# Attention by token tile with unnormalised P, and the convolution's inputs first in the odd projection

## What is computed

```python
z = h @ w_in
u_c = z[..., :2 * D_C]                              # 2 x 512, convolution: value and gate
q = rms_norm(z[..., o1:o2].reshape(B, T, 8, 64), q_g)
k = rms_norm(z[..., o2:o3].reshape(B, T, 2, 64), k_g)
v = z[..., o3:].reshape(B, T, 2, 64)
...
s = jnp.einsum('bqhgd,bkhd->bhgqk', qblk, k) * 64 ** -0.5
p = jax.nn.softmax(s, axis=-1)
o = jnp.einsum('bhgqk,bkhd->bqhgd', p, v)
...
g = val * jax.nn.sigmoid(gate)
y_c = silu(layer_norm(depthwise_conv(g, conv_w, conv_b, 15, 15)))   # 31 taps
y = jnp.concatenate([y_c, attn], axis=-1) @ w_out
```

## Time and profile before

| | |
|---|---|
| median of 3 runs | 2182.76 us (2178.67 to 2184.53) |
| the profiled execution | 2183.45 us, span 2181.8 us |
| TensorE busy | 1896.4 us, 87% of the span |
| DVE busy | 1391.6 us, 64% |
| ACT busy | 780.4 us, 36% |
| POOL busy | 268.7 us, 12% |
| chain that ended last | PE 73%, DVE 14%, issue 8%, ACT 2% |

### The profile page before, as it was taken

How to read it: one execution, slowest core, us unless ns; L and a number is a source line. 1 busy time by engine, 2 the same in 40 slices (tenths; PEclk the granted TensorE clock), 3 DMA queues, 4 the chain that set the end, 5 groups by cost and what they waited for, 6 DMA issues and landing times.

```text
span 2181.8 us, 34451 instructions
## 1 busy us (share of the span) xinstructions
PE 1896.4 (87%) x11818; PEld 1676.3 (77%) x11819; DVE 1391.6 (64%) x2732; ACT 780.4 (36%) x1297; POOL 268.7 (12%) x280
## 2 busy tenths in 40 slices
PE   4898899999999999977789767979797898797975
PEld 2694599999999999933336646979687898797974
DVE  1578745678888854389875472448576796684435
ACT  1425333221222223323323332336444565452321
POOL 1001100000000000089300010020101110101021
PEclk9999899999999999956779987989898998898996
DMA  7343224457744424200000132467757898866433
GB/s 225 116 150 121 78 75 121 134 153 231 205 136 125 148 66 138 69 19 3 0 1 10 36 106 80 118 188 211 207 158 208 244 253 242 232 177 174 116 90 129
DMA packets 439501, 288.76 MB, mean 132 GB/s; under 512 B 20858, under 2 KB 428634, under 8 KB 439300
## 3 DMA queue, kind: packets, MB, share of 16 engines
q1 hardware_dynamic: 425124, 248.75, 39.4%
q0 software_dynamic: 12272, 34.50, 5.1%
q10 hardware_dynamic: 1904, 3.13, 0.5%
HBM read 262.86 MB, written 23.47 MB: 131 GB/s over the span
## 4 chain that ended last, share of the span: by engine, by line
PE 73%; DVE 14%; issue 8%; ACT 2%; DMA 1%; ACTq 1%; DVEq 1%; POOL 0%; POOLq 0%
PE ps L1116 15%; PE ps L1117 15%; PE ps L1118 15%; PE ps L1121 11%; PE ps L1122 5%; DVE vp L2105 3%; PE ps L1228 2%; DVE lo L1727 2%; PE ps L1159 1%; PE ps L1441 1%; PE ps L1178 1%; PE ps L1458 1%; DVE am L2166 1%; DVE hot L2320 1%; ACT hi L700 1%
## 5 line engine op out<-in xcount | busy, mean ns | idle before, releaser
L700 ACT ACTIVATE hi<-raw 128x1024 fp32r<-128x1024 f32 (+3 forms) x442 | 397.1, 919 | 512.9 <-PE ps L1118 348.3
L1116 PE MATMUL ps<-h_wide,hi 128*128 128x320 f32 (+1 forms) x1728 | 542.2, 314 | 32.6 <-issue 26.5
L1117 PE MATMUL ps<-h_wide,hi 128*128 128x320 f32 (+1 forms) x1728 | 537.5, 311 | 0.0
L1118 PE MATMUL ps<-h_wide,lo 128*128 128x320 f32 (+1 forms) x1728 | 537.4, 311 | 0.0
L1727 DVE TENSOR_TENSOR lo<-raw,hi 128x1024 fp32r<-128x1024 f32 (+3 forms) x442 | 451.9, 1050 | 48.3 <-ACT hi L700 44.1
L1116 PEld LDWEIGHTS ps<-h_wide,hi 128*128 128x128 f32 x1728 | 327.8, 190 | 35.3 <-issue 33.1
L1121 PE MATMUL ps<-h_wide,hi 128*128 128x256 f32 (+2 forms) x1056 | 294.2, 364 | 61.8 <-issue 54.6
L1117 PEld LDWEIGHTS ps<-h_wide,hi 128*128 128x128 f32 x1728 | 327.4, 189 | 0.4 <-issue 0.2
L1118 PEld LDWEIGHTS ps<-h_wide,lo 128*128 128x128 f32 x1728 | 327.6, 190 | 0.0
L1121 PEld LDWEIGHTS ps<-h_wide,hi 128*128 128x128 f32 x1056 | 210.7, 200 | 68.5 <-issue 52.6
L1122 PE MATMUL ps<-h_wide,lo 128*128 128x128 f32 (+2 forms) x1056 | 258.0, 244 | 0.0
(11 more groups left out here) (337 smaller groups left out, 2459.2 us busy)
## 6 DMA issues: line engine op xcount, KB each, us to landing
raw<-in_moe_w_dram SPq DMA_DIRECT2D x160, 512.0 KB, 5.2
raw<-in_w_mod_dram SPq DMA_DIRECT2D x96, 512.0 KB, 4.6
raw<-in_moe_w_dram SPq DMA_DIRECT2D x64, 384.0 KB, 3.5
raw<-in_ff_w_dram SPq DMA_DIRECT2D x40, 512.0 KB, 4.7
raw<-in_moe_w_dram SPq DMA_DIRECT2D x64, 320.0 KB, 3.8
y_rows<-zeros POOLq DMA_DIRECT2D x22, 512.0 KB, 4.5
raw<-in_moe_w_dram SPq DMA_DIRECT2D x32, 256.0 KB, 2.9
raw<-in_ev_w_in_dram SPq DMA_DIRECT2D x12, 512.0 KB, 6.4
```

Source lines behind the costliest of these rows:

```text
L700: act.activation(hi[c % 2][:, parts[h]], raw[slot][:, parts[h]], ACT.Copy).then_inc(hi_done, 1)
L1116: pe.matmul(out, w_hi, v_hi, start=first, stop=False, skip_group_check=True)
L1117: pe.matmul(out, w_hi, v_lo, start=False, stop=False, skip_group_check=True)
L1118: return pe.matmul(out, w_lo, v_hi, start=False, stop=last, skip_group_check=True)
```

## The change

1. **Steps by token tile.** s = 8 t + h: first all eight heads of tile 0 (the context), then those of tile 1, and so on.
2. **P isn't divided.** ACT's exp takes P with scale -1 and the row minimum as bias (the q gain is multiplied by -1/8 once, at the start). The row sums of a tile's eight heads are kept, and the division is done on the output: `rows_out(t)` takes one reciprocal of eight and eight multiplications of 128 x 64, from PSUM. DVE's negation, reciprocal, multiplication of P and copy of the fifth tile are gone; ACT copies all five transposed tiles at once.
3. **P·V the other way round.** `weigh(s)` comes three steps behind the scores: P's transpose (128 x 128) is the weight, five of them a step (one for tile 0), and 64 columns of V are streamed, so queries are on the partitions of the result. `turn_back(t)` transposes a tile's 128 x 512 result with four transposes, and `rows_hi` and `rows_lo` write its high and low parts. Banks alternate by tile.
4. **The odd projection's order** is values and gates of the convolution first (chunks 3, 5, 4, 6), then q, k and v. DVE multiplies values by gates (`gated`) and does 22 taps between the chunks. POOL still waits for all four groups.

```diff
+ODD = (3, 5, 4, 6, 0, 1, 2)
...
-            for c in range(7):
-                split_hi(OIN + c + 2)
-                in_place(6 + c, c, z_odd)
+            for p in range(7):
+                split_hi(OIN + p + 2)
+                in_place(6 + p, ODD[p], z_odd)
...
             def kept(s):
 
-                h, t = s // TT, s % TT
                 act.wait_ge(a_t, s + 1)
-                if h >= 2:
-                    act.wait_ge(a_pv, h - 1)
-                if t == 0:
-                    act.activation(ptp[:, h % 2, :], ps[:, 4, 0:P], ACT.Copy).then_inc(a_kept, 1)
+                if s >= 2:
+                    act.wait_ge(a_pvs, s - 1)
+                if s < NH:
+                    act.activation(pt[:, s % 2, 0, :], ps[:, 4, 0:P], ACT.Copy).then_inc(a_kept, 1)
                 else:
-                    act.activation(pt[h % 2][:, 0:4, (t - 1) * P:t * P], ps[:, 4, 0:512].rearrange("p (k c) -> p k c", k=4),
+                    act.activation(pt[:, s % 2].rearrange("p k c -> p (k c)"), ps[:, 4:6, :].rearrange("p a b -> p (a b)")[:, 0:T],
                                    ACT.Copy).then_inc(a_kept, 1)
...
+            def rows_hi(t):
+                act.wait_ge(a_back, t + 1)
+                act.activation(hh[:, NC:KT, t * P:(t + 1) * P], ps[:, 6 + t % 2, :].rearrange("p (j c) -> p j c", j=NC), ACT.Copy).then_inc(a_ohi, 1)
...
-                    act.activation(dst, src, ACT.Exp, scale=HD ** -0.5, bias=am[:, 1, s % 2:s % 2 + 1],
-                                   accum_out=am[:, 2, s % 2:s % 2 + 1]).then_inc(a_exp, 1)
+                    if h == 0 and t >= 2:
+                        act.wait_ge(a_rows, t - 1)
...
+                    act.activation(dst, src, ACT.Exp, scale=-1.0, bias=am[:, t % 2, 0, h:h + 1],
+                                   accum_out=am[:, t % 2, 1, h:h + 1]).then_inc(a_exp, 1)
...
+            def weigh(s):
+
+                t, h = s // NH, s % NH
                 r = slice(HD * (h // 4), HD * (h // 4) + HD)
-                if k == 0:
-                    pe.wait_ge(a_kept, TT * (h + 1))
-                    pe.wait_ge(a_kept5, (TT - 1) * (h + 1))
-                    if h:
-                        pe.wait_ge(a_ohi, h)
-                        pe.wait_ge(a_olo, h)
-                    pe.matmul(ps[r, 7, 0:TP], vt[:, 0, r], ptp[:, h % 2, :], start=True, stop=True)
-                last = pe.matmul(ps[r, 6, 0:TS], vt[:, 1 + k, r], pt[h % 2][:, k, :], start=k == 0, stop=k == 4, skip_group_check=True)
-                if k == 4:
-                    last.then_inc(a_pv, 1)
+                at = P * (h % 4) + HD * (h // 4)
+                pe.wait_ge(a_kept, s + 1)
+                if h == 0 and t >= 2:
+                    pe.wait_ge(a_olo, t - 1)
+                tiles = 1 if t == 0 else 5
+                for k in range(tiles):
+                    last = pe.matmul(ps[:, 6 + t % 2, at:at + HD], pt[:, s % 2, k, :], vt[:, k if t == 0 else 1 + k, r], start=k == 0, stop=k == tiles - 1, skip_group_check=True)
+                last.then_inc(a_pvs, 1)
+
+            def turn_back(t):
+
+                pe.wait_ge(a_rows, t + 1)
+                for j in range(NC):
+                    last = pe.transpose(ps[:, 6 + t % 2, j * P:(j + 1) * P], o_rows[:, t % 2, j * P:(j + 1) * P], ident)
+                last.then_inc(a_back, 1)
...
-                if s >= 7:
-                    weigh((s - 7) // TT, (s - 7) % TT)
+                if 3 <= s < NH * TT + 3:
+                    weigh(s - 3)
+                if s >= NH + 5 and (s - 5) % NH == 0:
+                    turn_back((s - 5) // NH - 1)
...
+            dve.tensor_scalar(par[:, 1, QN:QN + 1], par[:, 1, QN:QN + 1], -HD ** -0.5, None, ALU.mult)
...
+            for p in range(7):
+                raw_out(6 + p, OIN + p, ODD[p], z_odd)
+                split_lo(OIN + p + 2)
+                if p in (2, 4):
+                    gated(p - 2)
+                    gated(p - 1)
+                if p >= 2:
+                    taps((4, 7, 4, 7, 0)[p - 2])
...
+            def rows_out(t):
+
+                slot = t % 2
+                dve.wait_ge(a_exp, NH * (t + 1))
+                link(dve.reciprocal(am[:, slot, 2, :], am[:, slot, 1, :]))
+                dve.wait_ge(a_pvs, NH * (t + 1))
+                if t >= 2:
+                    dve.wait_ge(a_back, t - 1)
+                for h in range(NH):
+                    at = P * (h % 4) + HD * (h // 4)
+                    last = dve.tensor_scalar(o_rows[:, slot, at:at + HD], ps[:, 6 + slot, at:at + HD], am[:, slot, 2, h:h + 1], None, ALU.mult)
+                last.then_inc(a_rows, 1)
...
+                if s >= NH + 4 and (s - 4) % NH == 0:
+                    rows_out((s - 4) // NH - 1)
+                if s >= NH + 7 and (s - 7) % NH == 0:
+                    rows_lo((s - 7) // NH - 1)
                 taps(2)
```

More of the change, by code:

```diff
@@ L76, in among @@
     return BY_PE.index(q) if q in BY_PE else q - sum(p < q for p in BY_PE)
-MANY = [(ring_of(OIN + c), 3) for c in range(2)] + [(ring_of(OOUT + c), 1) for c in range(4)]
+ODD = (3, 5, 4, 6, 0, 1, 2)
+MANY = [(ring_of(OIN + ODD.index(c)), 3) for c in range(2)] + [(ring_of(OOUT + c), 1) for c in range(4)]
 def landed(r):
@@ L365, in hybrid_trunk_step @@
         a_exp = sem("a_exp")
-        a_norm = sem("a_norm")
         a_t = sem("a_t")
         a_kept = sem("a_kept")
-        a_kept5 = sem("a_kept5")
-        a_pv = sem("a_pv")
+        a_pvs = sem("a_pvs")
+        a_rows = sem("a_rows")
+        a_back = sem("a_back")
         a_ohi = sem("a_ohi")
@@ L602, in q_columns, with odd_columns @@
                      src[:, k:k + 4, e, 2 * c + j, :]) for k in (0, 4) for j in range(2) for e in range(2)]
-            for c in range(2):
-                load(OIN + c, q_columns(c))
+            def odd_columns(c):
+                return q_columns(c) if c < 2 else columns(w, 2 * D_A + 512) if c == 2 else columns(w, (c - 3) * 256)
+            for p in range(2):
+                load(OIN + p, odd_columns(ODD[p]))
             sp.wait_ge(evac, 2 * OIN)
@@ L612, in _ @@
             sp.dma_start(hspread[:, :, :], a["const_hspread"]).then_inc(odd_in, 16)
-            load(OIN + 2, columns(w, 2 * D_A + 512))
-            for c in range(3, 7):
-                load(OIN + c, columns(w, (c - 3) * 256))
+            for p in range(2, 7):
+                load(OIN + p, odd_columns(ODD[p]))
             wo = a["od_w_out"][0]
@@ L1417, in turn @@
             def turn(s):
-                pe.wait_ge(a_norm, s + 1)
+                pe.wait_ge(a_exp, s + 1)
                 if s:
                     pe.wait_ge(a_kept, s)
[L1422 to L1427, removed]
+                for k in range(1 if s < NH else 5):
@@ L1445, in _ @@
+            def turn_back(t):
[3 more added lines that the diff above has]
+                last.then_inc(a_back, 1)
             pe.wait_ge(v_kept, 2)
             pe.wait_ge(o_rope, 5)
-            for s in range(NH * TT + 7):
-                if s < NH * TT:
-                    h, t = s // TT, s % TT
+            for s in range(NH * TT + 6):
+                t, h = s // NH, s % NH
+                if t < TT:
@@ L2080, in z_odd @@
                 return gp[:, m - 10, p0 + lo_t:p0 + hi_t]
[L2082 to L2093, removed]
             conv_w = GC_W - 30
@@ L2111, in taps, with gated @@
                 del todo[:n]
+            def gated(c):
+                dve.wait_ge(in_kept, 2 * (6 + 2 * (c // 2 + 1)))
+                for lo_t, hi_t, cond in SEGS:
+                    p0 = (GC_P, GC_S)[cond]
+                    last = dve.tensor_tensor(gp[:, c, p0:p0 + hi_t - lo_t], gp[:, c, p0:p0 + hi_t - lo_t], vp[:, c, lo_t:hi_t], ALU.mult)
+                last.then_inc(gp_set, 1)
+            dve.wait_ge(gp_pads, 1)
+            for p in range(7):
[6 more added lines that the diff above has]
+                    taps((4, 7, 4, 7, 0)[p - 2])
             taps(4)
@@ L2168, in _ @@
-                if 1 <= s < NH * TT + 1:
-                    u = s - 1
-                    width = P if u % TT == 0 else T
-                    dve.wait_ge(a_exp, u + 1)
-                    link(dve.reciprocal(am[:, 3, u % 2:u % 2 + 1], am[:, 2, u % 2:u % 2 + 1]))
-                    dve.tensor_scalar(pp[:, u % 2, 0:width], pp[:, u % 2, 0:width], am[:, 3, u % 2:u % 2 + 1], None, ALU.mult).then_inc(a_norm, 1)
-                if 2 <= s < NH * TT + 2 and (s - 2) % TT:
-                    u = s - 2
-                    h, t = u // TT, u % TT
-                    dve.wait_ge(a_t, u + 1)
-                    if h >= 2:
-                        dve.wait_ge(a_pv, h - 1)
-                    dve.tensor_copy(pt[h % 2][:, 4, (t - 1) * P:t * P], ps[:, 5, 0:P]).then_inc(a_kept5, 1)
@@ L2181, in _ @@
-                if s >= 12 and (s - 2) % TT == 0:
-                    head_lo((s - 12) // TT)
+                    if h == 0 and t >= 2:
+                        dve.wait_ge(a_exp, NH * (t - 1))
+                    low = am[:, t % 2, 0, h:h + 1]
+                    if t == 0:
```

(3 more changed lines are left out.)

50 lines of the change are left out of this document (19 added, 31 removed).

## The result

The changed kernel takes 2203.34 us (median of 7 runs, 2197.3 to 2208.56) against 2182.76 (7 runs, 2176.56 to 2189.86) beside it: ratio 1.0094, 95% interval 1.007 to 1.0117. It is 20.6 us slower; 2212 was forecast, 29 us slower, in a range of 2177 to 2227. The profiled execution has a span of 2201.7 us.

What follows compares the result with a forecast made beforehand. The prediction took TensorE as the bound, at a low clock in attention. Last scores +27.6 us and tail +1.5 made +29.1 on the profiled 2183.45 us: 2212 us, range 2177 to 2227.

Steps and rivals of the forecast that it cites:

- The clock: Attention: mixture too lean, so granted clock stays 0.50 from 945 to past the last scores, though TensorE never pauses.
- Rival 1: Attention: full clock is granted in tile 1 and stays, steps about 3.35 us, 2131 us in all; chance 0.11.
- A reading behind it: Before the attention, 945 to 967: TensorE busy 20.9 of 22 us, nearly all with 10-row weights, without the clock rising.
- The product: P·V in a full-tile step: ten load-bound records cost 2.3 us at 1.2 GHz, against 1.90 before.
- Rival 2: P·V product: loads hide in the streams, 1.26 us at 1.2 GHz, 2179 us in all, no change; chance 0.06.
- The transposes: Attention step: five transposes of P cost 1.26 us at 1.2 GHz, within a step of 5.99.
- the mark: Attention's end, the start of DVE's first mean subtraction: 1166.26 before, forecast 29.1 us later.
- Tile 0: Attention's first eight steps: 2.6 us each, 20.8 in all, with 2.18 for two convolution taps beside POOL.
- The tail: Last scores to DVE's first mean subtraction: 21.9 us against 20.4 before, +1.5.
- The projection: Odd projection's new order: last chunk's first half evicted some 4 us later, covered; were that cover gone, 1 to 4 us.
- The order's gain: Odd projection: the gatings leave the stage's end, but DVE waited there for the q/k sums anyway: nothing gained.
- The break-even: Attention: the change breaks even where 20 of the 32 long steps run at the low clock; below that it is faster.

Runs made afterwards that it cites:

- experiments 2 and 3: Changed kernel with 128 instead of 64 columns streamed per product record, in all heads or half; versions computing the whole attention took 2139.78 and 2147.54 us.
- burst_late_lo: Changed kernel plus eight extra fp32 512-column matmuls once, at tile 1's first product, and DVE's low part one step later; 2134.02 us in one run.
- experiment 6: As burst_late_lo, but four extra matmuls instead of eight; median 2175.62 us over ten executions.
- burst: Changed kernel plus eight extra fp32 512-column matmuls into a free bank, once, at tile 1's first product; 2193.9 us in one run.
- half_wide: Changed kernel with heads 0 to 3 streaming all 128 columns of V, heads 4 to 7 writing over the useless half; 2147.54 us, ratio to before 0.9828.
- late_lo: Changed kernel with only DVE's low part of a tile one step later, no extra matmuls; 2200.04 us in one run.
- burst4_late_lo: The kernel of experiment 6: four extra matmuls against eight in burst_late_lo; two executions of 2118 and 2124 us, eight of 2174 to 2183.
- wide_pairs: Changed kernel streaming V beside 64 zero columns, heads ordered 0, 4, 1, 5, ... so sharers of a PSUM stretch follow each other; 2139.78 us, ratio to before 0.9805.
- wide_v: Changed kernel streaming V beside 64 zero columns, head order unchanged; output differs; 2277.69 us, not comparable, first mean subtraction at 1122.40 instead of 1189.03.

## Why the forecast was right, and where it wasn't

- **The clock.** Right: 0.50 from the QK norm to past the last scores, with TensorE never idle from 1010 on. The reason held too: more columns behind the same loads bring it back (experiments 2 and 3). What the forecast lacked is that the level has a memory. It said that the mixture is too lean; the runs say that it is too lean to raise the clock from 0.50, but can keep it once it is up: from 1011 to 1090 in `burst_late_lo`, but not in every execution (experiment 6). Rival 1 (granted in tile 1 and kept) was thus nearer than its 0.11 and the reading of the earlier trace rows made it look: one burst and one wait away, in the executions that kept the clock. In the changed kernel as it stands a pause as in `burst` would probably have ended it.
- **A reading behind it.** One of the forecast's rows doesn't say what it took from it. TensorE's busy time in 945 to 967 isn't nearly all with 10-row weights: groups of that window, before the change, are

```profile
L1398 PE MATMUL ps<-hrs,hspread 10*128 10x320 f32 x19 | 11.4, 761 | 0.0
L1406 PE MATMUL ps<-qf,mats 128*128 128x512 f32 x8 | 8.3, 1142 | 0.0
```

  and 2.0 us more of the second kind for the keys. So about half of it was long streams through 128 rows, and the clock didn't rise. The experiments carry the conclusion without this row, but what exactly the clock follows stays open.
- **The product.** 2.16 us a step against 2.3, within its bounds of 1.26 and 2.5. Rival 2, loads hidden in the streams, falls: ten records take 1.23 us with 64 columns and 1.28 with 128, so the load is what is paid. The Trainium skill (TensorE: Matmul & The Clock Gate, LDWEIGHTS (loading the stationary operand)) would have a load of 128 columns in P / 1.2 ns, an estimate of 107 ns. The trace disagrees at the low clock and is near it at the high one: it has 0.216 us a record at 1.2 GHz (2.16 over ten) and 0.12 at 2.4.
- **The transposes.** Taken over at 1.26, they came to 1.12, as the next product's first load now runs beside the last transpose (it starts at 1036.17, the product at 1036.39). A step is 5.71, not 5.99, over 27 steps 7.6 us. The sums: the mark was forecast for 1195.4 (1166.26 + 29.1) and came 6.3 earlier. Up to the end of the scores of step 12 it is +4.1 (1011.6 instead of 1007.5), from there to the last scores -8.3 (157.7 us instead of 165.9; 7.6 of it is the shorter step, 0.7 isn't placed), and in the tail -2.1. So the total was nearer than its terms: two errors in opposite directions cancelled in part, which is luck.
- **Tile 0.** 3.0 us a step instead of 2.6, first minimum of tile 1 at 995.09 instead of 991.3. The term of the taps was too small: 2.18 for two was the mild case of the earlier trace rows; in the steps of tile 0 pairs took 3.24, 3.02 and 2.06. With the projection's 0.6 that makes +3.8, most of the +4.1.
- **The tail.** 19.8 us from the last scores (1169.2) to the mark, against 21.9: the mean sums took 5.40, not 6.6, as the clock came back within them, and the turns were shorter. The division's eight instructions took 1.62, 0.20 each instead of 0.15.
- **The projection.** The seven taps between the last chunks took 11.16 us, 1.6 each instead of 0.9, and the first minimum was at 971.16, 0.6 late: inside 0 to 4.
- **The order's gain.** "Nothing gained" held in the changed kernel and was wrong as a statement on the edit: with a wide V it is worth some 10 us, and alone it gives 0.9972, just clear of the noise.
- **The break-even.** The forecast's 20 slow steps of 32 can't be tested as such. With a mean clock of 0.77 the same attention (`half_wide`) is 35 us faster than before, the gain of the new order included.

## What to carry to other kernels

An edit that shortens what TensorE streams behind unchanged loads can take its clock away: look which level it has when the edited stage begins, and what the stage streams. Where columns are free behind a load, stream more of them, even into a place that is written over. And a short wait on another engine may cost far more than its length, where the work behind it can't bring the clock back: in `burst` a pause of 3.3 us went with a mark 64 us later than in `burst_late_lo`, in one execution of each.

## What the hardware showed

- A stage of matmuls can run at either of two levels with no difference in its own program, by what ran ahead of it: 39.00 of 39 us busy at 0.50, and 35.07 of 39 at 1.00, in `late_lo` and `burst_late_lo`.
- Without a pause TensorE stayed at 1.2 GHz for more than 150 us of back-to-back work, from 1010 to past the last scores at 1169. The Trainium skill (TensorE: Matmul & The Clock Gate, Loop structure matters more than you think) holds that dense work keeps the clock up; by that rule this kernel would have been faster than before, and the trace speaks against it where the clock has to rise. Where it is up already, `burst_late_lo` agrees (1.00 from 1011 to 1090), and the eight slower executions of `burst4_late_lo` don't.
- A tap on DVE (128x655) takes 0.9 us alone and up to 1.7 while POOL works on its own taps (a pair 1.83 us in the one case and 3.37 in the other, in the kernel after).
- In PSUM a product that adds to a stretch came out as meant where it followed that stretch's start directly (`wide_pairs`), and not where starts of other stretches of the same bank lay between (`wide_v`). What does it there is inferred from the outputs, not seen in a trace.
